# Two attention stages that each run their own output projection

## The reference, cut to what matters

```
def nsa_layer_mix(h, shared, mem_k, mem_v, w_in, w_out):
    q, gl, mq = split_cols(h @ w_in, [NSA_WIDTH, 3 * NSA_HEADS, MEM_WIDTH])
    gates = jax.nn.sigmoid(gl.reshape(B, T, NSA_HEADS, 3))
    o = nsa_attend(q, gates, *shared)            # compressed + selected + window attention, 8 heads of 64
    m = mem_attend(mq, mem_k, mem_v)             # 4 heads of 128 over 256 memory rows
    return jnp.concatenate([o, m], axis=-1) @ w_out          # (512 x 1024) @ (1024 x 1024)

# second block, per layer:
    o = gated_delta_rule_chunked(l2norm(heads(gq)), l2norm(heads(gk)), heads(gv), g, beta)
    o = rmsnorm_2(o, w_gdn_norm[l]) * jax.nn.silu(heads(gz).astype(f32))
    y_sb = stick_breaking_attention(sb_heads(sq), sb_heads(sk), sb_heads(sv)).reshape(Bsz, L, SB_WIDTH)
    x = x + jnp.concatenate([y_sc, y_gdn, y_sb], axis=-1) @ w_mix_out[l]
```

## Time and profile before

| | |
|---|---|
| median of 3 runs | 2007.61 us (2007.39 to 2008.82) |
| the profiled execution's own time | 2009.23 us |
| its span in the trace | 2007.5 us (27235 instructions) |
| PE busy | 1938.1 us, 97% of the span |
| DVE, ACT, POOL busy | 56%, 37%, 9% |

### The profile page before, as it was taken

One profiled execution on the slowest core, in us unless ns is written; L12 is line 12 of the kernel. 1 busy time (PEld: TensorE's weight loads), 2 busy tenths in 40 slices (PEclk: granted clock), 3 DMA queues, 4 the chain that ended last, 5 costly groups with the idle time before them and its releaser, 6 DMA issues. The chain is left out here.

```text
span 2007.5 us, 27235 instructions
## 1 busy us (share of the span) xinstructions
PE 1938.1 (97%) x10471; PEld 1584.3 (79%) x10471; DVE 1122.5 (56%) x1628; ACT 736.3 (37%) x1150; POOL 180.3 (9%) x178
## 2 busy tenths in 40 slices
PE   7999999999999988999999999999989999999998
PEld 7788788888788866578888788888768688888786
DVE  6435565565535547636556632667655466777532
ACT  7442542222324436524222332435433442222323
POOL 2201020000002005301000000200230020000001
PEclk9999999999999999999999999999998999999999
DMA  6311223333223610023333233323100223323221
GB/s 236 123 48 43 74 85 105 94 94 104 95 95 79 168 43 1 1 85 116 96 103 94 85 105 94 96 64 94 43 2 2 84 79 111 94 84 113 86 84 42
DMA packets 135495, 167.73 MB, mean 84 GB/s; under 512 B 28354, under 2 KB 102631, under 8 KB 135399
## 3 DMA queue, kind: packets, MB, share of 16 engines
q1 hardware_dynamic: 135219, 166.37, 26.8%
q10 hardware_dynamic: 180, 0.05, 0.0%
HBM read 164.29 MB, written 2.10 MB: 83 GB/s over the span
## 5 line engine op out<-in xcount | busy, mean ns | idle before, releaser
L195 PE MATMUL bank<-h_hi,w_hi 128*128 128x512 f32 x2192 | 860.8, 393 | 19.8 <-DVE h_lo L1672 6.3
L196 PE MATMUL bank<-h_lo,w_hi 128*128 128x512 f32 x2192 | 854.9, 390 | 0.0
L197 PE MATMUL bank<-h_hi,w_lo 128*128 128x512 f32 x2192 | 854.9, 390 | 0.0
L142 DVE TENSOR_TENSOR w_lo<-raw,w_hi 128x1024 fp32r<-128x1024 f32 x274 | 334.4, 1236 | 572.8 <-ACT w_hi L136 572.3
L195 PEld LDWEIGHTS bank<-h_hi,w_hi 128*128 128x128 f32 x2192 | 412.6, 188 | 114.8 <-issue 13.4
L136 ACT CAST w_hi<-raw 128x1024 fp32r<-128x1024 f32 x274 | 284.3, 1047 | 588.3 <-PE bank L195 579.8
L196 PEld LDWEIGHTS bank<-h_lo,w_hi 128*128 128x128 f32 x2192 | 412.6, 188 | 86.7 <-issue 1.9
L197 PEld LDWEIGHTS bank<-h_hi,w_lo 128*128 128x128 f32 x2192 | 412.4, 188 | 86.4
L1569 ACT ACTIVATE scratch<-scratch 128x512 f32<-128x512 f32 x66 | 41.8, 633 | 250.8 <-DVE scratch L1633 250.8
L326 POOL TENSOR_TENSOR tail<-keep 128x512 f32<-128x512 f32 x7 | 9.6, 1378 | 1224.2 <-ACT keep L310 1207.4
L1633 DVE SCALAR_TENSOR_TENSOR scratch<-keep,vecs,scratch 128x512 f32<-128x512 f32 x88 | 66.1, 752 | 10.8 <-DVE scratch L1632 1.7
(11 more groups left out here) (465 smaller groups left out, 1854.4 us busy)
## 6 DMA issues: line engine op xcount, KB each, us to landing
raw<-in_w_up SPq DMA_DIRECT2D x176, 256.0 KB, 3.0
raw<-in_w_down SPq DMA_DIRECT2D x44, 512.0 KB, 3.2
raw<-in_w_ffn_up SPq DMA_DIRECT2D x88, 256.0 KB, 3.3
raw<-in_w_mix_in SPq DMA_DIRECT2D x24, 512.0 KB, 3.7
raw<-in_w_ffn_down SPq DMA_DIRECT2D x22, 512.0 KB, 3.5
raw<-in_w_mem_kv SPq DMA_DIRECT2D x16, 512.0 KB, 5.0
raw<-in_a_w_in SPq DMA_DIRECT2D x16, 512.0 KB, 3.7
raw<-in_a_w_out SPq DMA_DIRECT2D x8, 512.0 KB, 3.9
```

Of the source, the lines that this page charges most:

```text
L142: dve.tensor_tensor(k.w_lo[n % RING][:, :], k.raw[n % RING][:, :], k.w_hi[n % RING][:, :].bitcast(F32), ALU.subtract)\
L195: a = pe.matmul(out, sh, mh, start=first, stop=False)
L196: pe.matmul(out, sh, ml, start=False, stop=False)
L197: c = pe.matmul(out, sl, mh, start=False, stop=last)
```

## The change

- `stage_out_projection` is gone. `stage_nsa` and `stage_delta` take in its work on every engine, so each loses one block barrier.
- `stage_nsa`: SP streams the remaining weight chunks from the start of the stage. PE does the 24 matmuls of the first weight chunk (feature tiles 0 and 1) after step m = 8 of the last pair; chunks 1 to 3 follow the last `values_mem`, then the second group.
- `stage_delta`: results of the recurrence go to banks 4 to 7 (`bk`), which leaves banks 0 to 3 to the projection. ACT halves the four weight chunks before it squares; DVE does its part of chunks 0 and 1 inside the recurrence, chunk 2 after it, chunk 3 after the gating. The first four chunks come in the feature order 0,1 / 6,7 / 2,3 / 4,5. `stick_values(1)` moves from after c = 2 to after c = 3. PE does chunk 0, then the four sums of squares, then chunks 1 to 3 and the second group. The five dummy products are gone. Gated outputs, squares and `rstd` move to other tiles.

```diff
-def pe_group(k, pe, t, tiles, h_from=None, aside=None, rstd_by=None, order=tuple(range(8)), bank_free=None):
+def pe_group(k, pe, t, tiles, h_from=None, aside=None, rstd_by=None, order=tuple(range(8)), bank_free=None,
+             ready=None, chunks=range(4)):
...
-            pe.wait_ge(k.h_ready.sem, k.h_ready.at(h_from + order.index(kk) + 1))
+            pe.wait_ge(k.h_ready.sem, k.h_ready.at(h_from + (ready or order).index(kk) + 1))
...
-    for c in range(4):
+    for c in chunks:
...
-def stage_out_projection(k, gain, split=False):
...
-def stage_nsa(k):
+def stage_nsa(k, gain):
...
+    first = k.ring.took
+    ho = k.handoff = Handoff(k, rounded=8)
...
+        @blk.sync
+        def _(sp):
+            stream(k, sp, first + 8)
...
+            def out_bank_free(i):
+                if i == 0:
+                    pe.wait_ge(zc_read, 8)
+                elif i == 2:
+                    pe.wait_ge(me_done, 16)
+
+            out_tiles = [feature_tile(k, m * P) for m in range(4)]
...
                     elif m == 8:
                         values_sel(j, (2, 3))
+                        if j == 3:
+                            pe_group(k, pe, 0, out_tiles, 0, bank_free=out_bank_free, ready=order, chunks=(0,))
...
             values_mem(3)
+            pe_group(k, pe, 0, out_tiles, 0, ready=order, chunks=(1, 2, 3))
+            pe.wait_ge(fin, 4)
+            pe.wait_ge(finm, 4)
+            pe_group(k, pe, 4, out_tiles)
...
             dve_split(k, dve, value, 6, tiles=order[6:8])
+            out_projection_dve(k, dve, ho, gain, first)
...
+            pool_sums(k, pool, ho, range(1, 4), 7)
...
             act_split(k, act, value, None, tiles=order[6:8])
+            out_projection_act(k, act, ho, gain, first)
...
-def stage_delta(k, a):
+DELTA_ORDER = (0, 1, 6, 7, 2, 3, 4, 5)
+def stage_delta(k, a, gain):
...
+    bk = lambda i: bank(k, i + 4)
...
-    o_sb, osq, rstd = heads(0), Lm, heads(6144)
+    o_sb, osq, rstd = k.catT[:, 2:6, :], ck, cq
...
+    k.phase_end = k.next_end
     first = k.ring.took
+    ho = k.handoff = Handoff(k, rounded=8)
...
-            stream(k, sp, first)
+            stream(k, sp, first + 8)
...
-                if c == 2:
-                    stick_values(1)
-            pe.wait_ge(tr, 16)
-            for h in range(H):
-                pe.wait_ge(o_sq, h + 1)
-                if h == 3:
-                    pe.wait_ge(vc, 2)
-                pe.matmul(bank(k, 4 + h)[:, :], k.ones[:, :], osq[:, h, :], start=True, stop=True).then_inc(o_nf, 1)
-            pe.wait_ge(o_rd, 1)
-            pe_warm(k, pe, 5, 4)
+            stick_values(1)
+
+            def out_bank_free(i):
+                if i == 0:
+                    pe.wait_ge(vr, 4)
+                elif i < 3:
+                    pe.wait_ge(tr, 16)
+                else:
+                    pe.wait_ge(vc, 2)
+
+            def head_sums():
+                for h in range(H):
+                    pe.wait_ge(o_sq, h + 1)
+                    pe.wait_ge(o_gated, h + 1)
+                    pe.matmul(bk(h)[:, :], k.ones[:, :], osq[:, h, :], start=True, stop=True).then_inc(o_nf, 1)
+
+            t = pe_group(k, pe, 0, [feature_tile(k, m * P) for m in range(4)], 0, aside=(1, head_sums), order=DELTA_ORDER,
+                         bank_free=out_bank_free)
+            pe.wait_ge(o_rd, H)
+            pe_group(k, pe, t, [feature_tile(k, m * P) for m in range(4)])
...
             weights(1, 3)
-            finish(1)
+            act.wait_ge(xf, 6 * G2)
+            act.wait_ge(vf, 1)
+            split_hi(k, act, first + 4)
+            act.wait_ge(ws, C - 1)
+            act_split(k, act, lambda kk: k.catT[:, kk, :], None, tiles=(0, 1))
             act.wait_ge(of, 1)
             for h in range(H):
-                act.activation(osq[:, h, :], bank(k, h)[:, :], ACT.Square, scale=P ** -0.5).then_inc(o_sq, 1)
+                act.activation(osq[:, h, :], bk(h)[:, :], ACT.Square, scale=P ** -0.5).then_inc(o_sq, 1)
+            finish(1)
+            act.wait_ge(vc, 2)
+            act.wait_ge(df, C - 1)
+            act_split(k, act, lambda kk: k.catT[:, kk, :], None, tiles=(6, 7))
             for h in range(H):
                 act.wait_ge(o_nf, h + 1)
...
                 act.activation(rstd[:, h, :], rstd[:, h, :], ACT.Exp, scale=-0.5).then_inc(o_rd, 1)
+                if h >= 2:
+                    act.wait_ge(normed, 2 * (h - 1))
+                    act_split(k, act, lambda kk: k.catT[:, kk, :], None, tiles=(2 * h - 2, 2 * h - 1))
+            out_projection_act(k, act, ho, gain, first)
...
+            pool_sums(k, pool, ho, range(1, 4), 7)
...
+                if c == 1:
+                    split_lo(k, dve, first + 2)
                 if c < C - 1:
...
                         dve.tensor_copy(S[0][:, :, :], d).then_inc(sr, 1)
+                        split_lo(k, dve, first + 1)
...
-            dve.wait_ge(vc, 2)
+            dve.wait_ge(vr, C)
+            dve_split(k, dve, lambda kk: k.catT[:, kk, :], 0, tiles=(0, 1))
+            split_lo(k, dve, first + 3)
+            dve.wait_ge(vf, 2)
             for h in range(H):
...
+            dve_split(k, dve, lambda kk: k.catT[:, kk, :], 2, tiles=(6, 7))
+            split_lo(k, dve, first + 4)
             for h in range(H):
                 dve.wait_ge(o_rd, h + 1)
                 dve.wait_ge(o_gated, h + 1)
-                dve.tensor_tensor(k.catT[:, 2 + h, :], o_sb[:, h, :], rstd[:, h, :], ALU.mult)
+                dve.tensor_tensor(k.catT[:, 2 + h, :], o_sb[:, h, :], rstd[:, h, :], ALU.mult).then_inc(normed, 1)
+                if h == 3:
+                    dve_split(k, dve, lambda kk: k.catT[:, kk, :], 4, tiles=(2, 3, 4, 5))
+            out_projection_dve(k, dve, ho, gain, first)
...
-        (False, [plain(a["w_mix_out_2"][0], cols) for cols in (0, 512)], [lambda: stage_delta(k, a)]),
+        (False, [reordered(a["w_mix_out_2"][0], DELTA_ORDER), plain(a["w_mix_out_2"][0], 512)], [lambda: stage_delta(k, a, gain_of(k, "w_norm_ffn_2"))]),
```

More of the change, by code:

```diff
@@ L2694, in decayed @@
                     cs = slice(c * P, (c + 1) * P)
-                    mm = pe.matmul(bank(k, h)[:, cs], ck[:, h, cs], k.kbeta[:, h, cs], start=True, stop=True)
+                    mm = pe.matmul(bk(h)[:, cs], ck[:, h, cs], k.kbeta[:, h, cs], start=True, stop=True)
                 mm.then_inc(kkf, 1)
@@ L2703, in other @@
                     if n < 4:
-                        mm = pe.matmul(bank(k, 4)[:, cs], ck[:, n, cs], cq[:, n, cs], start=True, stop=True)
+                        mm = pe.matmul(bk(4)[:, cs], ck[:, n, cs], cq[:, n, cs], start=True, stop=True)
                     else:
-                        mm = pe.transpose(bank(k, 4)[:, cs], (ck, cv)[n % 2][:, (n - 4) // 2, cs], k.ident[:, :])
+                        mm = pe.transpose(bk(4)[:, cs], (ck, cv)[n % 2][:, (n - 4) // 2, cs], k.ident[:, :])
                 mm.then_inc(othf, 1)
@@ L2711, in halves @@
                     for r in (upper, lower):
-                        mm = pe.matmul(bank(k, b)[r, cs], stat[r, cs], mov[r, cs], start=True, stop=True)
+                        mm = pe.matmul(bk(b)[r, cs], stat[r, cs], mov[r, cs], start=True, stop=True)
                 return mm
@@ L2718, in turn @@
                     for r in (upper, lower):
-                        mm = pe.matmul(bank(k, g)[r, cs], Lm[r, g, cs], k.ident[r, r], start=True, stop=True)
+                        mm = pe.matmul(bk(g)[r, cs], Lm[r, g, cs], k.ident[r, r], start=True, stop=True)
                 mm.then_inc(yf, 1)
@@ L2743, in corner_first @@
                 for i, cs in enumerate(blocks):
-                    mm = pe.matmul(bank(k, g)[lower, cs], corner(g)[upper, i, lower], X[upper, g, cs], start=True, stop=True)
+                    mm = pe.matmul(bk(g)[lower, cs], corner(g)[upper, i, lower], X[upper, g, cs], start=True, stop=True)
                 mm.then_inc(yf, 1)
@@ L2751, in corner_second @@
                 for i, cs in enumerate(blocks):
-                    mm = pe.matmul(bank(k, 2 + g)[upper, cs], Y[lower, g, cs], whole(g)[lower, i, lower], start=True, stop=True)
+                    mm = pe.matmul(bk(2 + g)[upper, cs], Y[lower, g, cs], whole(g)[lower, i, lower], start=True, stop=True)
                 mm.then_inc(xf, 1)
@@ L2760, in stick_scores @@
                     for r, b in ((upper, 5), (lower, 6)):
-                        mm = pe.matmul(bank(k, b)[:, c - j * P:c - j * P + P], k.sbk[r, p, j * P:(j + 1) * P], k.sbq[r, p, c:c + P],
+                        mm = pe.matmul(bk(b)[:, c - j * P:c - j * P + P], k.sbk[r, p, j * P:(j + 1) * P], k.sbq[r, p, c:c + P],
                                        start=True, stop=True)
@@ L2872, in _ @@
                         pe.wait_ge(w_out, (n - 5) // 2 + 1)
-                b = bank(k, (n + 4) % 5)
+                b = bk((n + 4) % 5)
                 for c in range(C):
@@ L2888, in _ @@
                     for h in range(H):
```

(12 more changed lines are left out.)

45 lines of the change are left out of this document (23 added, 22 removed).

## The result

The changed kernel takes 1992.48 us in the median of four runs (1992.13 to 1992.52), the kernel before 2008.21 us beside it (2007.39 to 2009.68). The ratio is 0.992, with a 95% interval of 0.9903 to 0.9938: faster by 15.7 us (12.5 to 19.5 by that interval). The forecast was 1992.0, its range 1989.8 to 1996.0. The profiled executions differ by a little more, 2009.23 against 1992.46 us, with spans of 2007.5 and 1990.8. A part of such differences is the TensorE clock, which wasn't the same in all traces of the same code; the experiments show how much.

What follows compares the result with a forecast made beforehand. The prediction took PE, working 97% of the span, as the bound, so only idle or slow PE could be won. 4.8 + 10.9 = 15.7 us off 2007.6 gave 1991.9, rounded 1992.0, range 1989.8 to 1996.0.

Steps and rivals of the forecast that it cites:

- First junction: End of the sparse-attention stage and start of its projection: 4.8 us won.
- 3.1 of pause: PE's idle time between the sparse-attention stage's last products and its projection, 3.1 us, goes away.
- 1.7 of slow clock: First eleven steps of the sparse-attention projection take 4.19 us where 2.50 would do; this 1.7 us goes away.
- Second junction: Delta stage from c = 2 to the projection's last matmul: 63.8 us becomes 52.7; after two costs, 10.9 won.
- the wait before c = 3: Delta recurrence: PE idles uncovered until the state of c = 2 is ready, 0.7 us.
- the 167 steps: Chunks 1 to 7 of the delta projection on PE, at 0.2269 us a step: 37.9 us.
- Two costs of 0.1: Delta stage: a 0.1 us stall for tile 2, and 0.1 for DVE's remainder of chunk 1 inside the recurrence.
- three terms (0.7, 0.1 and 0.1): Second junction's wait before c = 3 and its two costs; the range's lower end assumed that they vanish, 1.6 us less.
- Rival 1: The slow clock moves to fresh small pauses instead of going: 1.7 to 2.9 us lost, 1993.7 to 1996.5; chance 0.16.
- Rival 2: Tile 3, tile 2 or the recurrence later than counted: 1 to 4 us lost, 1993 to 1996; chance 0.11.
- Rival 3: PE's clock falls before the second merged stretch and stays low through the delta projection: 38 us, 2030; chance 0.03.
- Rival 4: The pause before the following stage grows by what was won: no effect, 2007.6; chance 0.02.

Runs made afterwards that it cites:

- dummies in the pause: Kernel before, with three float32 dummy products on PE at the very end of the sparse-attention stage: 2005.77 us for 2008.76, ratio 0.9985.
- the delta part alone: Kernel before, with only the delta stage taking in its projection, sparse attention and its projection left as before: 1998.11 us, ratio 0.9947.
- the last kernel: Changed kernel with chunk 0 after step 6, `stick_values(1)` after c = 2, its copy before the squares, two dummy products before the recurrence: 1993.34 us, ratio 0.9925.
- the kernel without dummies: Changed kernel with chunk 0 after step 6 of the last pair, `stick_values(1)` after c = 2 and its copy before the squares: 1990.22 us, ratio 0.9914.

## Why the prediction was right

**First junction, 4.8 us:** 4.77. Its two terms, 3.1 of pause and 1.7 of slow clock, came out as 3.2 and 1.6 with dummies in the pause. Chunk 0 costs nothing by itself, as I said; that its place behind step 8 gains nothing either was implied, and moving it behind `values_mem` showed it (55.82 for 55.87). In front of turn 7, where PE waits, its place is worth 1.0 us.

**Second junction, 10.9 us:** 10.86 where both traces have a low clock in the recurrence (76.08 to 65.22). Term by term, predicted and measured: the wait before c = 3 0.7 and 0.61; L2880 to the first product of chunk 0, 1.9 + 1.0 + 2.3 = 5.2, and 1555.82 - 1550.49 = 5.33; chunk 0 5.4 and 5.59; sums 3.5 and 3.43; the 167 steps 37.9 and 37.87. For the last two the recorded starts mislead: L2907 to the first product of chunk 1 is 3.03 us, and that product to the next 0.63 (1564.44 to 1565.07). The last of the eight float32 instructions hasn't had its 0.43 us when the first product is on record as started; 3.03 + 0.63 is 8 x 0.43 and one step of 0.227. All terms together are 52.8 for the predicted 52.7. Two costs of 0.1 did not come: tile 2 was ready with 0.4 us to spare (its remainder 8.4 us after the first sum, where I had counted 9.0), and DVE's two halvings inside the recurrence moved nothing. From the first new values to L3226 of c = 1 it is 3.67 us and to L3237 5.61; the kernel before has the same 3.67 and 5.61 in the trace with dummies in the pause, which also has the full clock there.

**Where luck helped.** The old delta interval that I had read, 76.08, was the longest of three; the two others are 73.55. With these, and the full clock in the recurrence on both sides, the second junction is 73.55 - 63.90 = 9.65, and both together 14.4 instead of 15.7. The interval of the measured difference, 12.5 to 19.5 us, holds both. So the mechanism and the terms are shown, but that the median moved by just 15.7 is in part chance. My own range also had a slip: its lower end takes off 1.6 us for three terms (0.7, 0.1 and 0.1) that add up to 0.9.

**Rival 1, a slow stretch that moves:** right in part. The fresh pause that I feared, 0.61 us before c = 3, was followed by the full clock. But slow stretches that were there before do come and go, and it cuts both ways. The recurrence had the low clock in 6 of 13 traces without dummies there, behind the same 2.13 us of idle; it costs 1.3 us (65.22 to 65.37 against 63.90). The start of the old delta projection had 2.9 us of slow clock in the trace that I read and 1.7 in two others: 76.08 less 1.3 and less 1.2 is the 73.55 found there. That the profiled spans differ by 16.7 and not 15.7 is this: 4.77 + 10.86 + 1.3 for the recurrence = 16.9, and the rest of the span lost 0.2. These 13 traces are of eleven kernels. The changed kernel itself had the full clock in the recurrence in all three of its traces, so whether each execution draws anew there, or the edits further ahead decide it, is not shown. Elsewhere identical kernels do differ; the changed kernel in its first profile and in its second:

```profile
720.00:725.00 5.00, 5.00 (x23) 4.16 (x23) 2.04 (x3) 1.12 (x2) 0.00 (x0) 1.00 0.23 56
720.00:725.00 5.00, 4.99 (x15) 3.96 (x16) 2.10 (x3) 1.91 (x6) 0.00 (x0) 0.66 0.10 7
```

The Trainium skill, "TensorE: Matmul & The Clock Gate", section "What's actually happening", says that the gate's windows run freely, so that the point at which the clock switches varies; it says so of the rise at a kernel's start. These two rows agree with a clock that switches at other places from one execution to the next.

**Rival 2, late tails:** tile 3 and tile 2 were in time with 0.4 us or more. It is a question of order: with the plain one, PE waits 5.0 us and 7.7 are lost. **Rival 3, slower:** nothing of it; the clock read 1.00 in both merged projections of the changed kernel. **Rival 4, no effect:** both barriers at the end of the merged stages still cost PE 0.47 us, as before, and gave nothing back.

**Still open:** what decides the clock in the recurrence, and whether dummies in front of it pay.

## What to carry to other kernels

Where one engine is busy 97% of the time, look for a stage border at which it waits for the last tiles of the stage and let it start the next product with tiles that are ready: here that removed the pause and the slow clock behind it. What decides is the order in which the contraction takes its tiles; here the order was worth 7.7 us, the place of the first chunk nothing, except in front of a turn that PE waits for (1.0 us). Compare variants by an interval between two instructions of the trace, and only at the same clock. The sparse interval was 55.86 to 55.91 us in seven traces with the same code there, while the whole time of the unedited changed kernel spread over 0.4, 2.3 and 5.7 us in its three sets.

## What the hardware showed that I had not expected

PE's idle time of 2.13 us before the recurrence was followed by a low clock in 6 of 13 traces (granted clock 0.57 in the kernel before, 0.58 in the delta part alone) and by the full clock in the other 7, so the same stage code differs by 1.3 us. The times of whole executions scatter more. The profiled one of the last kernel took 1987.45 us at a mean granted clock of 0.995, that of the kernel without dummies 1995.18 at 0.988; their own intervals differ by only 1.4. From 10 to 20 us, far ahead of any edit, the clock was 1.00 in the first and 0.66 in the second. Small edits can't be judged by such totals.
